# First stage of a decoder trunk on one core: token differences and five value mixes on GpSimd, two key tiles chunk by chunk in turn, eight places for the squares of x

## The reference, cut to what matters

```python
def rms_norm(x, gain, eps=RMS_EPS):
    y = xf * lax.rsqrt(jnp.mean(xf * xf, axis=-1, keepdims=True) + eps)
    return (y * gain)

# rwkv7_time_mix(h = rms_norm(x, mix_norm[0]), ...)
xx = jnp.pad(h, ((0, 0), (1, 0), (0, 0)))[:, :-1] - h      # previous token minus this one
x_mix = h[None] + xx[None] * mu[:, None, None, :]           # six mixes
rkv = jnp.einsum('cbsd,cde->cbse', x_mix[:3], w_rkv)        # receptance, key, value
xw, xa, xg, xv = x_mix[3], x_mix[4], x_mix[5], x_mix[2]     # decay, a, gate use the others
...
```

## Time and profile before

| | us |
|---|---|
| median of 3 runs | 1872.77 (1872.58 to 1875.38) |
| profiled execution, its own time | 1873.18 |
| its span | 1871.4 |
| TensorE busy | 1802.8 |
| VectorE, ScalarE, GpSimd busy | 912.0, 769.5, 195.0 |

### The profile page before, as it was taken

One profiled execution on the slowest core, in us unless ns is written; L12 is line 12 of the kernel. 1 busy time (PEld: TensorE's weight loads), 2 busy tenths in 40 slices (PEclk: granted clock), 3 DMA queues, 4 the chain that ended last, 5 costly groups with the idle time before them and its releaser, 6 DMA issues.

```text
span 1871.4 us, 36223 instructions
## 1 busy us (share of the span) xinstructions
PE 1802.8 (96%) x15618; PEld 1378.7 (74%) x15618; DVE 912.0 (49%) x1561; ACT 769.5 (41%) x1309; POOL 195.0 (10%) x172
## 2 busy tenths in 40 slices
PE   8989999979999999999999999999999899999999
PEld 3745555556558888888888788788787688888887
DVE  6725555546454444433454654655555454444321
ACT  4434443443243233222446656666656533323211
POOL 0033333333000000000011111111110000000000
PEclk9999999999999999999999999999999999999999
DMA  3311111121113323323322222222221132332332
GB/s 118 118 55 61 63 58 64 58 92 58 36 58 112 101 90 101 102 91 100 99 82 79 80 68 91 80 73 75 79 80 56 57 101 91 102 101 91 101 102 90
DMA packets 57542, 155.01 MB, mean 83 GB/s; under 512 B 5591, under 2 KB 22535, under 8 KB 57384
## 3 DMA queue, kind: packets, MB, share of 16 engines
q1 hardware_dynamic: 57288, 152.63, 25.6%
q10 hardware_dynamic: 96, 0.07, 0.0%
HBM read 150.51 MB, written 11.61 MB: 87 GB/s over the span
## 4 chain that ended last, share of the span: by engine, by line
PE 68%; ACT 3%; DVE 1%; issue 1%; ACTq 0%; DVEq 0%
PE bank L537 66%; PE bank L540 2%; ACT f L1520 2%; DVE f L2012 0%; ACT f L1507 0%; ACT f L1533 0%; ACT r L1498 0%; ACT f L1494 0%; ACT f L1525 0%; DVE r L1884 0%; DVE f L1607 0%; DVE f L2005 0%; DVE r L1596 0%; ACT r L1211 0%; ACT L1474 0%
## 5 line engine op out<-in xcount | busy, mean ns | idle before, releaser
L537 PE MATMUL bank<-r 128*128 128x512 f32 x5424 | 1256.3, 392 | 5.4 <-DVE r L2029 3.7
L537 PEld LDWEIGHTS bank<-r 128*128 128x128 f32 x5424 | 1014.6, 188 | 228.0 <-issue 15.7
L537 PE MATMUL bank<-f 64*64 64x64 f32 (+5 forms) x9762 | 513.0, 259 | 50.2 <-ACT f L1286 15.6
L537 PEld LDWEIGHTS bank<-f 64*64 64x64 f32 (+3 forms) x9762 | 315.7, 143 | 234.8 <-issue 120.2
L1596 DVE TENSOR_TENSOR r<-f,r 128x1024 fp32r<-128x1024 f32 x222 | 274.9, 1239 | 399.0 <-ACT r L1211 399.0
L1211 ACT ACTIVATE r<-f 128x1024 fp32r<-128x1024 f32 x222 | 232.6, 1048 | 148.6 <-PE bank L537 141.2
L2181 POOL TENSOR_TENSOR r<-f,r 128x512 fp32r<-128x512 f32 x48 | 62.1, 1294 | 845.1 <-ACT r L1498 845.1
L1477 ACT ACTIVATE r<-f 128x512 fp32r<-128x512 f32 x44 | 27.8, 632 | 215.6 <-DVE f L1923 215.6
L1953 DVE TENSOR_TENSOR f<-bank,f 128x512 f32<-128x512 f32 x72 | 56.2, 780 | 73.4 <-PE bank L537 70.1
L1727 DVE TENSOR_TENSOR f<-bank,f 64x512 f32<-64x512 f32 x80 | 55.0, 688 | 64.7 <-PE bank L537 63.5
L540 PE MATMUL bank<-f 128*128 128x128 f32 x432 | 64.8, 280 | 9.9 <-DVE f L2012 8.4
(11 more groups left out here) (105 smaller groups left out, 921.4 us busy)
## 6 DMA issues: line engine op xcount, KB each, us to landing
f<-stream SPq DMA_DIRECT2D x245, 512.0 KB, 3.5
bias_copies<-bias_rows SPq DMA_DIRECT2D x6, 1536.0 KB
f<-xT SPq DMA_DIRECT2D x16, 256.0 KB, 4.5
f<-lora_out SPq DMA_DIRECT2D x16, 128.0 KB, 5.3
f<-bias_copies SPq DMA_DIRECT2D x16, 128.0 KB, 3.2
f<-bias_copies SPq DMA_DIRECT2D x32, 64.0 KB, 3.0
outT<-f SPq DMA_DIRECT2D x8, 256.0 KB, 4.3
f<-wo_last SPq DMA_DIRECT2D x2, 512.0 KB, 6.0
```

Source lines behind the costliest of these rows:

```text
L537: return nc.tensor.matmul(out, lhsT, rhs, start=start, stop=stop, skip_group_check=True)
```

## The change

- Squares of x are written to eight places (the receptance buffer O_A, free at this time); ScalarE no longer waits for TensorE.
- GpSimd computes the eight differences xx, and the value mixes of chunks 0 to 4, as an addition of h to mu2 * xx, which ScalarE makes (`scaled_difference`). VectorE makes the value mixes of chunks 5 to 7 inside its receptance loop, at i = 2, 3, 4. VectorE's second loop is gone.
- Both key tiles go chunk by chunk in turn. Their two panels must both be there at the start.
- The value panel goes to a place of its own (the value buffer O_VIN), so SyncE issues it at once behind panel 1 and the small constants. The value tile uses bank 5.
- VectorE makes the low half of the first receptance panel at i == 6 instead of 3. ScalarE's program mixes roundings, scaled copies and takes in another order.

```diff
-                mm(NORM_SUM[:, :], con(C_ONES), f(O_TMP + k % 2 * S), k == 0, k == KC - 1).then_inc(s["x_norm_ps"], 1)
+                mm(NORM_SUM[:, :], con(C_ONES), f(O_A + k * S), k == 0, k == KC - 1).then_inc(s["x_norm_ps"], 1)
...
+                if p == PAN_V:
+                    sp.dma_start(f(O_VIN, 1024), stream[p]).then_inc(s["w_v"], 16)
+                    return
...
-            plain(PAN_K, O_MIXK, "mix_k")
-            plain(PAN_K + 1, O_MIXK, "mix_k")
+            for t in (PAN_K, PAN_K + 1):
+                raw_in(pe, t)
+            for c in range(KC):
+                pe.wait_ge(s["mix_k"], c + 1)
+                for t in (PAN_K, PAN_K + 1):
+                    last = mm(banks[t][:, :], raw(t, c), f(O_MIXK + c * S), c == 0, c == KC - 1)
+                    if c == KC - 1:
+                        last.then_inc(s["dense"], 1)
...
-            plain(PAN_V, O_MIXV, "mix_v")
+            pe.wait_ge(s["w_v"], 16)
+            for c in range(KC):
+                pe.wait_ge(*((s["mix_v"], c + 1) if c < N_MIXV else (s["mix_v_late"], c - N_MIXV + 1)))
+                last = mm(banks[5][:, :], f(O_VIN + c * P, P), f(O_MIXV + c * S), c == 0, c == KC - 1)
...
-                if k >= 2:
-                    act.wait_ge(s["x_norm_ps"], k - 1)
-                A(f(O_TMP + k % 2 * S), hk(k), ACT.Square).then_inc(s["sq"], 1)
+                A(f(O_A + k * S), hk(k), ACT.Square).then_inc(s["sq"], 1)
...
+            def scaled_difference(k):
+                act.wait_ge(s["xx"], k + 1)
+                A(f(O_MIXV + k * S), f(O_XX + k * S), ACT.Identity, scale=vec("mu2", k)).then_inc(s["mu_v"], 1)
+
             for k in range(KC):
                 act.wait_ge(s["h"], k + 1)
...
+                if k in (3, 4, 6, 7):
+                    scaled_difference((3, 4, 6, 7).index(k))
...
+            round_mixed(0)
+            scaled_difference(N_MIXV - 1)
+            round_mixed(1)
             take(PAN_K, O_KIN)
             take(PAN_K + 1, O_KIN + S)
+            round_mixed(2)
...
-            for i in range(3):
+            for i in (3, 4):
                 round_mixed(i)
             split_high(PAN_R)
-            round_mixed(3)
+            for i in range(5, KC):
+                round_mixed(i)
             take(PAN_V, O_VIN)
-            for i in range(4, KC):
-                round_mixed(i)
...
-            for k in range(KC + 1):
-                if k < KC:
-                    dve.wait_ge(s["mix_k"], k + 1)
-                    TT(f(O_XX + k * S), hk(k, 1), hk(k), ALU.subtract).then_inc(s["xx"], 1)
-                if k:
-                    dve.wait_ge(s["xx"], k)
-                    STT(f(O_MIXV + (k - 1) * S), f(O_XX + (k - 1) * S), vec("mu2", k - 1), hk(k - 1),
-                        ALU.mult, ALU.add).then_inc(s["mix_v"], 1)
...
+                if j == 0:
+                    dve.wait_ge(s["xx"], k + 1)
...
-                if i == 3:
+                if 2 <= i < KC - N_MIXV + 2:
+                    k = i - 2 + N_MIXV
+                    dve.wait_ge(s["xx"], k + 1)
+                    STT(f(O_MIXV + k * S), f(O_XX + k * S), vec("mu2", k), hk(k), ALU.mult, ALU.add)                        .then_inc(s["mix_v_late"], 1)
+                if i == 6:
                     split_low(PAN_R)
...
+            def difference(k):
+                pool.wait_ge(s["mix_k"], k + 1)
+                TT(f(O_XX + k * S), hk(k, 1), hk(k), ALU.subtract).then_inc(s["xx"], 1)
+
+            def mix_value(k):
+                pool.wait_ge(s["mu_v"], k + 1)
+                TT(f(O_MIXV + k * S), f(O_MIXV + k * S), hk(k), ALU.add).then_inc(s["mix_v"], 1)
+
+            difference(0)
+            for k in range(N_MIXV - 1):
+                difference(k + 1)
+                mix_value(k)
+            for k in range(N_MIXV, KC):
+                difference(k)
+            mix_value(N_MIXV - 1)
```

More of the change, by code:

```diff
@@ L303, in trunk @@
         MIXED_AT = {PAN_R + 4 + n: [KC + 2 * n, KC + 2 * n + 1] for n in range(4)}
+        N_MIXV = 5
         NORM_TMP = [O_NT0, O_NT1, O_NT1]
@@ L422, in raw_in @@
         def raw_in(eng, p):
-            early = p > PAN_WA and (p - PAN_WA) % RAW == 0
-            eng.wait_ge(s[f"w_raw{p % RAW}"], 16 * (p // RAW + 1 - early))
+            apart = sum(p > q and (p - q) % RAW == 0 for q in (PAN_V, PAN_WA))
+            eng.wait_ge(s[f"w_raw{p % RAW}"], 16 * (p // RAW + 1 - apart))
         def full(eng, t):
@@ L445, in panel @@
             def panel(p):
-                held = p - RAW - (RAW if p - RAW == PAN_WA else 0)
+                held = p - RAW - (RAW if p - RAW in (PAN_V, PAN_WA) else 0)
+                if p == PAN_V:
+                    sp.dma_start(f(O_VIN, 1024), stream[p]).then_inc(s["w_v"], 16)
+                    return
                 if p == PAN_WA:
@@ L1243, in _ @@
                 A(f(O_XX + k * S), hk(k), ACT.Identity, scale=f(O_SM + 48 + k, 1)).then_inc(s["h_part"], 1)
+                if k in (3, 4, 6, 7):
+                    scaled_difference((3, 4, 6, 7).index(k))
             def take(t, off, func=ACT.Copy):
                 full(act, t)
-                A(f(off), banks[t % 2][:, :], func).then_inc(freed(t), 1)
+                A(f(off), banks[5 if t == PAN_V else t % 2][:, :], func).then_inc(freed(t), 1)
+            round_mixed(0)
+            scaled_difference(N_MIXV - 1)
+            round_mixed(1)
             take(PAN_K, O_KIN)
             take(PAN_K + 1, O_KIN + S)
+            round_mixed(2)
             for g in range(3):
```

## The result

| | before | changed |
|---|---|---|
| median, 8 runs each | 1875.18 us (1872.19 to 1876.61) | 1880.18 us (1877.75 to 1880.64) |
| ratio | | 1.0027, 95% interval 1.0017 to 1.0037 |
| profiled execution: span | 1871.4 us | 1878.8 us |

The change makes the kernel slower by 5.0 us, 0.27% (by the interval 3.2 to 6.9 us). The forecast was +3.7 us, that is 1876.5 us, with a range of 1869.3 to 1880.6. The measured 1880.18 lies 3.7 above the forecast: 2.4 of it is the kernel before, whose 8 runs have a median of 1875.18 where the forecast started from 1872.77, and 1.3 is the change.

A forecast was written before the change was run, and what follows sets the result against it. VectorE was taken to bound the first stage: from 14.2, 22.1 us own work plus 12.4 waiting gives 48.7, then 5.48 and 0.1 give 54.2 against 50.43. Taken as +3.7 on 1872.77: 1876.5 us, range 1869.3 to 1880.6.

The forecast's parts named there:

- VectorE paces the stage: First stage, before the receptance tiles: VectorE, hardly ever idle from 15.21 us on, sets the pace, not TensorE.
- the unbroken run: TensorE's 168 back-to-back matmuls from the second receptance tile: start forecast at about 54.2 us instead of 50.43.
- Squares: Sum of squares of x at the start: eight places let VectorE start at 14.2 instead of 15.21, gain 1.0 us.
- Turn of GpSimd: First stage: each of 13 GpSimd operations makes VectorE wait 0.95 us, 12.4 us in all, bounds 10.5 and 16.3.
- the lower bound 0.81: Lowest assumed VectorE wait in us per GpSimd operation, from a 1.06 us one; gives +1.9 instead of +3.7 us.
- The signs that the prediction named for the turns: Key loop: about seven of sixteen VectorE operations at 1.5 to 1.7 us, last mix_k about 31.5; GpSimd from 16.5 to 41.
- VectorE's own count: VectorE's work up to the first receptance panel's low half, without waits for GpSimd: 10.6 + 8.3 + 2.0 + 1.18 = 22.1 us.
- rival C: TensorE, starved before the receptance tiles, falls to the lower clock and loses 1.7 us there: 1878.2 us, chance 0.18.
- A: The forecast case: VectorE and GpSimd alternate in the first stage, no second clock loss; 1874.0 to 1880 us, chance 0.55.
- Rival B: First stage: GpSimd does not hold VectorE up, TensorE sets the pace; 2.8 to 3.9 us earlier, about 1869.5, chance 0.13.
- Key tiles in turn and the value panel ahead: First stage: sixteen key products, 13.8 us, keep up with VectorE's 1.33 us a chunk; the earlier value panel costs nothing.
- D: First-stage change does not reach the end, or low-clock stretches in later stages offset it: 1872.8 us, chance 0.14.

The follow-up runs named there:

- the kernel without GpSimd's part: Changed kernel with differences and all value mixes back on VectorE, ScalarE's copies gone, first split at i == 3: 1874.74 us, ratio 1.0000 to before.
- the run with the additions: Kernel before plus 13 GpSimd additions of 128x512 that read SBUF, results unused: 1887.92 us against 1874.75, ratio 1.0065.
- the fills: Kernel before plus 26 GpSimd fills of 128x512 that write SBUF and read nothing: 1874.52 us, ratio 0.9997.

## Why the prediction was right, point by point

- **VectorE paces the stage; the point to watch is the start of the unbroken run.** Right. Forecast for the first receptance tile 48.7, measured 48.46, and the kernel without GpSimd's part is back at 1.0000. This agreement of 0.2 us is luck: it comes of errors that cancel, the next three. That the measured median lies within the range, 0.4 us under its upper end, owes much to the range's width: 11.3 us, about twice the effect.
- **Squares, -1.0 us.** Wrong, they give 0.0. The step took the weight load at 7.26 for the start of a product. It was loaded ahead, while the product before it still ran. In the changed kernel TensorE is busy from 6.37 without a break, 14 records in 7.29 us, so the landing of x's second chunk and TensorE's own eight products set the norm. The old waits for a place were almost wholly beside that queue.
- **Turn of GpSimd, 0.95 us.** The mechanism was right, the size too large: 0.78 in the run with the additions, just under the lower bound 0.81 that the L2106 row gave. The mistake was the choice of row. L2106 is a subtraction, as eight of the new ones are, and takes 1.06 alone; the new ones take 1.04 (subtraction) and 1.09 (addition) where nobody disturbs them. L2144 and L2100 take 1.27 and were the wrong neighbours. The changed kernel's own turns are a little dearer than 0.78 where the addition is the one in place: VectorE's starts at 23.75, 25.19 and 26.69 give 1.44 - 0.66 = 0.78 beside L2085 and 1.50 - 0.66 = 0.84 beside L2089. All 13 come to 10.7 us by the next point, 0.82 each, where the forecast had 12.4: 1.7 us too much. The signs that the prediction named for the turns came: seven turns in the key loop, its last mix done at 31.9 (forecast 31.5), GpSimd's work from 17.5 to 40.3. The Trainium skill's rule (SBUF — State Buffer, Who interferes with whom), that two SBUF inputs on VectorE exclude a GpSimd instruction that reads SBUF and not one that only writes, was borne out in both halves by the additions and the fills; priced with whole durations it would have been further off still.
- **VectorE's own count, 22.1 us.** From 15.15 to 48.37, the end of the low half (it starts at 47.15 and lasts 1.22), are 33.2 us. The 22.1 leave out 0.4: the prediction reads 11.0 us for the key loop, start-up and end with their short waits for ScalarE's copies, and puts 8 x 1.33 = 10.6 into the sum. 33.2 - 22.1 - 0.4 = 10.7 are the turns. So the three errors are +1.0 from the squares, -1.7 from the turns and +0.4 here, together -0.3: 48.4 instead of 48.7.
- **Clock, rival C.** It was given 0.18 and it came, on top of A: forecast 1.7 us in the receptance tiles, measured 1.63 by its removal. This is why the result is +5.0 and not +3.7. The forecast itself, A, was "no second clock loss", so on this point the less likely rival was right. The sum of A's part alone (53.9 for the second receptance tile without the lower clock, 48.46 + 5.47, against 50.43) is +3.5.
- **Rival B** fell: VectorE got no second turn ahead of a waiting GpSimd in 13 turns.
- **Key tiles in turn and the value panel ahead: nothing.** Right, by the kernel without GpSimd's part. (Making the low half at i == 6 instead of 5 is 1.27 us of the loss, by the run that moved it.)
- **The end keeps the shift (against D).** The medians say 5.0 and the low-rank tile 5.1. The two profiled spans differ by 7.4; the last section says where the rest lies, as far as is known.

## What to carry to other kernels

Before moving work from VectorE to GpSimd, count the VectorE operations beside it that read two SBUF tiles: against those, each GpSimd operation costs VectorE more (0.78 to 0.84 us here) than the operation saved (0.63), and records of doubled length with no idle time are the sign. Put one input of the VectorE operations into PSUM, or the GpSimd work beside operations that read PSUM, and the same move can win: here the ratio went from 1.0027 to 0.9980. And price a wait ahead of a busy stretch of TensorE at more than its length, since a stretch at the lower clock can follow (1.63 us here).

## What the runs showed of the hardware that was not expected

A starved TensorE can stay at the lower clock level for long. In the kernel with the 13 additions the granted clock was 0.50 throughout a stretch in which TensorE was busy three quarters of the time (windows of TensorE):

```profile
17.00:20.00 3.00, 0.38 (x1) 0.53 0.00 0
20.00:30.00 10.00, 7.61 (x8) 0.50 0.00 0
30.00:40.00 10.00, 7.55 (x9) 0.50 0.00 0
40.00:42.00 2.00, 2.00 (x4) 0.73 0.19 41
```

It rose at about 41, with TensorE at work without a break from 36.87 on.

Later stretches at the lower clock differ between the two profiled executions as well. The same stretch of the first head, 5.1 us apart in the two kernels, has it in the changed kernel and not before (windows of TensorE, changed, then before):

```profile
136.00:141.00 5.00, 2.87 (x41) 1.00 0.43 131
141.00:145.00 4.00, 4.00 (x55) 0.57 0.02 4
```

```profile
131.00:136.00 5.00, 2.87 (x51) 1.00 0.42 131
136.00:140.00 4.00, 4.00 (x111) 1.00 0.02 4
```

A stretch of 3.4 us at half speed costs up to 1.7 us. Between 60 and 410 us the changed kernel's trace has five of them and that of the kernel before four. That is one part of the 2.4 us by which the profiled spans differ beyond the medians' 5.0. The executions themselves say as much: the one that was profiled before the change took 1873.18, 2.0 under the median of its eight, the other 0.5 over its own. Whether the shift of 5 us decides which stretches fall to the lower clock is not shown; no run shifts the work and changes nothing else.
